# Loads of three stages issued one stage ahead, and the keys' bias rows written by ScalarE

## The reference, cut to what matters

```python
def even_mixer(h_lat, h_ctx, w_in, q_gain, k_gain, f_gain, w_fmix, w_out, cos, sin, need_ctx):
    q, ga, k, v, u, gb = jnp.split(h @ w_in, EVEN_SPLITS, axis=-1)   # for context and latents
    q, k = rms_norm(q, q_gain), rms_norm(k, k_gain)                   # 12 query heads, 4 key heads of 64
    ql, kl = apply_rope(ql, cos, sin), apply_rope(kl, cos, sin)
    attention: context on itself, latents on all 2304 keys
    fourier_mix: un = rms_norm(u, f_gain); fft2(un, axes=(1, 3)).real; per group @ w_fmix
    y = concat([a * silu(ga), f * silu(gb)]) @ w_out
x = layer_norm(ALPHA * x + g * y) * post_ln_gain + post_ln_bias
```

## Time and profile before

| | us |
|---|---|
| median of 3 runs | 3640.65 |
| lowest, highest | 3634.57, 3640.83 |
| the profiled execution, device time | 3631.57 |
| its span, first to last instruction | 3629.8 |
| heads stage in it | 574.4 to about 691 |
| Fourier stage in it | 1792.6 to about 1858.1 |
| mixer out, first instruction | 1858.34 |
| TensorE busy, share of the span | 93% |
| VectorE, GpSimd, ScalarE busy | 65%, 51%, 37% |

### The profile page before, as it was taken

How to read it: one execution, slowest core, us unless ns; L and a number is a source line. 1 busy time by engine, 2 the same in 40 slices (tenths; PEclk the granted TensorE clock), 3 DMA queues, 4 the chain that set the end, 5 groups by cost and what they waited for, 6 DMA issues and landing times. The chain is left out here.

```text
span 3629.8 us, 49706 instructions
## 1 busy us (share of the span) xinstructions
PE 3375.2 (93%) x16176; PEld 2487.3 (69%) x16176; DVE 2377.5 (65%) x3519; ACT 1348.9 (37%) x2266; POOL 1841.1 (51%) x1240
## 2 busy tenths in 40 slices
PE   7999997799999999999779899799999998999798
PEld 5788884555555555555368689687878786877587
DVE  4666533778777777777647654466575645777566
ACT  3423333444444444444320033334343423654200
POOL 1033305477777777777434334323586513444354
PEclk9999997899999999999889999999999999999899
DMA  5345437411111111111245455564545446677563
GB/s 211 110 117 141 132 92 222 149 33 35 35 35 35 36 39 38 35 35 35 80 151 176 158 179 175 197 199 147 171 132 171 146 148 213 210 225 241 195 221 137
DMA packets 358864, 475.35 MB, mean 131 GB/s; under 512 B 57964, under 2 KB 212476, under 8 KB 358544
## 3 DMA queue, kind: packets, MB, share of 16 engines
q1 hardware_dynamic: 299024, 357.32, 31.6%
q10 hardware_dynamic: 53200, 95.64, 8.7%
q0 software_dynamic: 6448, 19.94, 1.4%
HBM read 337.32 MB, written 135.36 MB: 130 GB/s over the span
## 5 line engine op out<-in xcount | busy, mean ns | idle before, releaser
L2371 DVE TENSOR_REDUCE al_mx<-al_sx 128x1 f32<-128x512 f32 (+1 forms) x960 | 559.7, 632 | 201.6 <-PE al_sx L2474 191.9
L2291 ACT ACTIVATE al_e<-al_st 128x1024 f32<-128x1024 f32 x432 | 443.3, 1027 | 535.3 <-PE al_st L2489 535.1
L2340 POOL TENSOR_TENSOR al_acc_p<-al_acc_p,al_e 128x1024 f32<-128x1024 f32 x188 | 455.5, 2423 | 19.5 <-POOL al_acc_p L2334 0.5
L274 PE MATMUL pb_acc<-p_whi,pb_r_hi 128*128 128x512 f32 x952 | 379.4, 398 | 39.7 <-DVE pb_r_lo L1708 28.8
L2498 PE MATMUL al_acc<-al_e,vres 128*64 128x512 f32 x1728 | 402.5, 601 | 0.0
L276 PE MATMUL pb_acc<-p_whi,pb_r_lo 128*128 128x512 f32 x952 | 376.7, 396 | 0.0
L275 PE MATMUL pb_acc<-p_wlo,pb_r_hi 128*128 128x512 f32 x952 | 376.0, 395 | 0.0
L1708 DVE TENSOR_TENSOR pb_r_lo<-pb_stg,pb_r_hi 128x512 fp32r<-128x512 f32 x238 | 249.8, 1053 | 166.9 <-ACT pb_r_hi L1606 162.6
L2488 PE MATMUL al_st<-al_qa,kres 128*128 128x512 f32 x864 | 346.8, 401 | 3.8 <-issue 3.2
L2489 PE MATMUL al_st<-al_qb,kres 128*128 128x512 f32 x864 | 341.0, 395 | 0.0
L2474 PE MATMUL al_sx<-kres,al_qx 128*128 128x512 f32 (+1 forms) x960 | 310.9, 397 | 8.8 <-DVE al_mx L2371 7.2
(11 more groups left out here) (345 smaller groups left out, 7384.8 us busy)
## 6 DMA issues: line engine op xcount, KB each, us to landing
pb_stg<-s_hsum ACTq DMA_DIRECT2D x238, 256.0 KB, 2.8
s_proj<-pb_out SPq DMA_DIRECT2D x72, 256.0 KB, 3.3
p_wst<-in_w1s ACTq DMA_DIRECT2D x18, 1024.0 KB, 5.8
ml_k<-s_proj SPq DMA_DIRECT2D x36, 512.0 KB, 4.4
ml_v<-s_proj SPq DMA_DIRECT2D x36, 512.0 KB, 8.8
hm_w<-in_ada_w SPq DMA_DIRECT2D x16, 1024.0 KB, 8.8
ml_qt<-s_qt SPq DMA_DIRECT2D x32, 512.0 KB, 6.4
s_h<-ml_h POOLq DMA_DIRECT2D x32, 512.0 KB, 8.2
```

The source lines that it names most:

```text
L274: nc.tensor.matmul(out, s_hi, m_hi, start=start, stop=False)
L2291: nc.scalar.activation(e[:, pair(p, j), :, :], st[(NP * p + j) % 2][:, :, 0:W], ACT.Exp).then_inc(e_done, 1)
L2340: nc.gpsimd.tensor_tensor(acc_p[:], acc_p[:], e[:, pair(p, j)], ALU.add).then_inc(add_p, 1)
L2371: V.tensor_reduce(mx[:, x:x + 1], slots[x % NSX][:, 0:spans[x % NS][1]], AX.X, ALU.max).then_inc(sx_max, 1)
```

## The change

Three objects now own inputs of a later stage, and their loads are issued in the stage before.

- `HeadInputs` lies at the right end of SBUF from the first stage on. Its weight ring `hm_w` takes the place of half 1 of the projections' `whi` and `wlo`, its raw rows that of the tile `x`, its gains and rope rows that of the query heads' `turn`. At k = 76 of the projections SP waits until the query heads are through with them (`tr_done`, `sq_done`, `px_done`, `ss_done`, `turn_done`) and for `mm_done` of chunk 3, and loads the gains; from k = 76 to 83 it loads, in turn, 4 tiles of raw and rope rows and 4 pieces of `ada_w`.
- In the heads stage SP starts with the modulation's constants and the first context queries. The gains are no longer loaded by ScalarE's queue.
- GpSimd's `bias_rows` is gone. ScalarE writes the 8 half rows as copies of one column of the identity, 2 in each of rounds 0, 1, 2 and 1 in each of rounds 3, 4, ahead of `high_part`.
- `FourierInputs`: SP loads `u` in one DMA and all tables before the last pair of stores of the attention.
- In the Fourier stage the scratch tiles `ep`, `em`, `op`, `om` lie in the mixer's input tile and `side` lies in `four`; the output weights get 3 slots instead of 2, and their high parts begin at y = 3. SP loads the mixer's first two tiles (`MixerInputs`) after `odd_done`, between output weights 2 and 3.
- Mixer out starts without the four loads of its first two tiles.

```diff
@@ class HeadInputs (new)
+        with ExitStack() as shared:
+            self.split = [shared.enter_context(nc.sbuf_tensor(n, [P, KD, CH], F32R, side="right"))[:] for n in ("pj0_whi1", "pj0_wlo1")]
+        self.w = right("hm_w", [P, self.ROWS, KD // 2, CH])
+        self.x = right("hd_x", [P, 3 * D])
+    def load_rows(self, eng, n):
+        i = n % self.ROWS
+        eng.dma_start(self.raw[:, i, :], self.s["proj0"][n * P:(n + 1) * P, QW:C_GATE]).then_inc(self.ld[i], 16)
+        eng.dma_start(self.rope[:, i], self.a["rope"][n * P:(n + 1) * P]).then_inc(self.ld[i], 16)
@@ projections, SP
+                n = k - (K - 14)
+                if n == 0:
+                    for done, count in ((hq.tr_done, NT), (hq.sq_done, NT), (hq.px_done, NT), (hq.ss_done, NT), (hq.turn_done, 2 * NT)):
+                        sp.wait_ge(done, count)
+                    sp.wait_ge(mm_done, last_of[NCH - 2] + 1)
+                    head.load_gains(sp)
+                if 0 <= n < 8 and n % 2 == 0:
+                    for i in (NT + n // 2, 2 * NT + n // 2):
+                        sp.wait_ge(stored[i % NST], 16 * (i // NST) + 16)
+                    head.load_rows(sp, n // 2)
+                elif 0 <= n < 8:
+                    l, c = HEAD_CHUNKS[n // 4]
+                    head.load_weights(sp, n // 2, (l, c, n // 2 % 2))
@@ heads, SP
-            load(0)
             sp.dma_start(mod.sel[:], a["mod_sel"]).then_inc(mod.const, 16)
             sp.dma_start(mod.sil[:], s["sil"]).then_inc(mod.const, 16)
+            ca.load(sp, 0)
             for n in range(NR_RAW):
-                if n:
-                    load(n)
                 mod.load(sp, n)
-            ca.load(sp, 0)
@@ heads, ScalarE
+            def bias_rows(i):
+                at = i % 2 * (T // 2)
+                nc.scalar.activation(kres[HD:P, NKV + i // 2, at:at + T // 2], keep["ident"][HD:P, HD:HD + 1].broadcast_to([P - HD, T // 2]), ACT.Copy).then_inc(rows_done, 1)
-            act.dma_start(gk[:], a["qk_gain"][:, QW:QW + HD].broadcast_to([P, HD])).then_inc(gain_ld, 16)
-            act.dma_start(gf[:], a["f_gain"].broadcast_to([P, FW])).then_inc(fgain_ld, 16)
             squares(0)
             for n in range(NT):
                 if n + 1 < NT:
                     squares(n + 1)
+                for i in ((0, 1), (2, 3), (4, 5), (6,), (7,))[n] if n < 5 else ():
+                    bias_rows(i)
                 if n:
                     high_part(n - 1)
@@ heads, GpSimd
-            def bias_rows(h, i):
-                x = kres[:, NKV + h, i * (T // 2):(i + 1) * (T // 2)].bitcast(F32)
-                nc.gpsimd.memset(x[HD:P], 0.0).then_inc(rows_zero, 1)
-                pool.wait_ge(rows_zero, 2 * h + i + 1)
-                nc.gpsimd.memset(x[HD:HD + 1], 1.0).then_inc(rows_done, 1)
@@ attention, SP
             over_blocks(sp, body)
+            following.load(sp)
             store(TOTAL - 2, TOTAL // 2 - 1)
@@ class FourierInputs (new)
+        sp.dma_start(self.u[:], self.s["un"].rearrange("(t p) n -> p t n", p=P)).then_inc(self.u_ld, 16)
+        sp.dma_start(self.small[:, 0:2, :], self.a["dft_head"].rearrange("c p n -> p c n")).then_inc(self.small_ld, 16)
+        sp.dma_start(self.small[:, 2:4, :], self.a["fmix"].rearrange("c p n -> p c n")).then_inc(self.small_ld, 16)
+        sp.dma_start(self.tabs[0][:], self.a["dft_ctx"]).then_inc(self.small_ld, 16)
+        sp.dma_start(self.tabs[1][:], self.a["dft_lat"]).then_inc(self.tab_ld, 16)
@@ fourier, SP
-            sp.wait_ge(u_ld, 48)
-            sp.dma_start(tabs[1][:], a["dft_lat"]).then_inc(tab_ld, 16)
-            for k in range(2):
+            for k in range(out_weights.depth):
                 out_weights.load(sp, k)
-            for k in range(2, KD):
+            sp.wait_ge(odd_done, 1)
+            for i in range(2):
+                mixer.load(sp, i, slice(i * P, (i + 1) * P))
+            for k in range(out_weights.depth, KD):
                 out_weights.load(sp, k)
@@ fourier, ScalarE
-                if y >= 4 and k < KD:
+                if y >= 3 and k < KD:
@@ mixer_out, SP
             def before():
-                inputs(0, 0, 0)
-                inputs(1, 1, 0)
+                if not L0:
+                    inputs(0, 0, 0)
+                    inputs(1, 1, 0)
                 constants()
@@ program
-    out_weights, four = OutWeights(nc, m, 0, a["w_out0"], 2), m.sb("four", [P, 2, T])
+    out_weights, four, mixer_in = OutWeights(nc, m, 0, a["w_out0"], 3), m.sb("four", [P, 2, T]), MixerInputs(m, s)
```

More of the change, by code:

```diff
@@ L197, with __init__ @@
+HEAD_CHUNKS = [(0, 4), (0, 5)] + [(1, c) for c in range(6)]
 class FirstInputs:
-    def __init__(self, m, a):
-        self.a = a
+    def __init__(self, m, a, head):
+        self.a, self.head = a, head
         self.hall = m.sb("pj0_hall", [P, KD, NT, P])
         self.wst = m.sb("pj0_wst", [P, KD // 2, CH])
-        self.x = m.sb("pj0_x", [P, 3, D])
+        self.x = head.rows
         self.w1_st = self.hall[:, 0:KD // 2, NT - 4:, :].rearrange("p k t n -> p k (t n)")
@@ L700, in _ @@
                 hq.load_gain(sp)
-            for k, (c, t) in enumerate(steps):
+            for k, (_, t) in enumerate(steps):
+                c = steps[k][0]
                 if c == 0 and t == 0:
@@ new lines, with __init__, load @@
+class MixerInputs:
+    def __init__(self, m, s):
+        self.s = s
+        self.ins = m.sb("mo0_in", [P, 2, 2, D])
+        self.in_ld = m.sem("mo0_in_ld", 2)
+        self.sems, m.sems = m.sems, []
+    def load(self, sp, p, rows):
+        sp.dma_start(self.ins[:, p, 0, 0:QW].rearrange("p (k n) -> p k n", n=P), self.s["attn"][:, rows].rearrange("(k p) n -> p k n", p=P)).then_inc(self.in_ld[p], 16)
+        sp.dma_start(self.ins[:, p, 1, :].rearrange("p (k n) -> p k n", n=P), self.s["gt"][:, rows].rearrange("(k p) n -> p k n", p=P)).then_inc(self.in_ld[p], 16)
@@ L2587, in fourier @@
+def fourier(nc, m, a, s, keep, out_weights, four, early, mixer):
     jobs = ((0, CT, "dft_ctx"), (CT, LT, "dft_lat"))
     H, Q = LT // 2, LT // 4
-    u = m.sb("fo_u", [P, NT, FW])
+    u, small, tabs = early.u, early.small, early.tabs
+    m.sems += early.sems
     ev, od = m.sb("fo_ev", [P, H - 1, FW]), m.sb("fo_od", [P, H - 1, FW])
-    ep, em, op, om = (m.sb("fo_" + x, [P, Q - 1, FW]) for x in ("ep", "em", "op", "om"))
-    side = m.sb("fo_side", [P, 14, FW])
+    ep, em, op, om = (mixer.ins[:, i // 2, i % 2, 0:(Q - 1) * FW].rearrange("p (t n) -> p t n", n=FW) for i in range(4))
+    sides = [four[:, i // 9, i % 9 * FW:(i % 9 + 1) * FW] for i in range(14)]
@@ L2782, in _, with mixer_out @@
                 mixed(n)
-def mixer_out(nc, m, a, s, keep, layer, out, out_weights, following=None, four=None):
+def mixer_out(nc, m, a, s, keep, layer, out, out_weights, following=None, four=None, early=None):
     L0 = layer == 0
@@ L2830, in inputs @@
                     sp.wait_ge(y_done[p], v)
-                elif not (isinstance(n, int) and n < 2):
+                else:
                     sp.wait_ge(lo_done, n - 1)
```

146 lines of the change are left out of this document (83 added, 63 removed).

## The result

The changed kernel takes 3605.7 us (median of 5 runs, 3598.7 to 3616.4), the kernel before 3640.8 in the same comparison: a ratio of 0.9914, 95% interval 0.990 to 0.9928. The forecast was 3602, and 3587 to 3616 its range. The profiled execution of after took 3605.7 with a span of 3604.0; that of before had a span of 3629.8, on a run (3631.6) 9 us under its kernel's median. So the two profiles differ by 25.8 us where the medians differ by 35, and the forecast's own sum, −38.2 between profiles, was 12 us too large.

A forecast was written before the change was run, and what follows sets the result against it. TensorE fills 93% of the span, so gains lie in late stage starts and heads' early rounds. Heads −18, attention +0.5, Fourier −15, mixer −5.7 give −38.2 us: 3593.4 profiled, 3602 as median, range 3587 to 3616.

The forecast's parts named there:

- What bounds the kernel: TensorE fills 93% of the span; late starts in heads, Fourier and mixer out lie on the path.
- Heads, start: −4.1: Start of heads: inputs are there at opening, so ScalarE's first copy comes 4.1 us earlier.
- Heads, rounds 0 to 5: 21.3 us: Heads: without GpSimd's memsets rounds follow ScalarE, scalings running from 580.1 to 601.4; round 5 comes 20.7 us earlier.
- Heads, rounds 5 to 17: 64 us: Heads: 58 us at VectorE's pace, plus 5 for TensorE's low clock (0 to 10) and 1 for DMA engines (0 to 5).
- rival B: Heads: low clock in rounds 2 to 8 and 2.1 us bias copies leave −8, 3612; chance 0.25 together with the DMA rival.
- my own sign for B: Heads: scalings in rounds 5 to 12 over 5.5 us apart, with TensorE back to back at 1.2 GHz.
- Projections: 0: Last 14 projection steps: 6 MB of added loads and the wait at k = 76 cost nothing.
- rival D: Last 14 projection steps: loads ahead of stores stall TensorE each step, making the kernel slower by over 0.2%; chance 0.02.
- End of attention: +0.5: End of attention: last store waits behind five loads of 4.98 MB, costing 0.5 us, bounds 0 and 3.
- Fourier −15.0 and mixer −5.7: Fourier: earlier start and output weights, −15.0 us; mixer out: first product 0.3 us after start instead of 6.0, −5.7.
- the tail −20.2: Terms after heads: end of attention +0.5, Fourier −15, mixer out −5.7.

The follow-up runs named there:

- heads_late: Changed kernel with gains, row tiles 0 to 3, their ropes and weight pieces 0 to 3 loaded when heads opens again: 3615.5 us, ratio 0.9949 to the kernel before.
- before_rows_act: Kernel before with only the bias rows moved from GpSimd's memsets to ScalarE copies, all loads left in place: 3632.2 us, ratio 0.9991 to the kernel before.
- aligned128: Changed kernel with 96 unused bytes at the right end of SBUF: 3597.9 us, ratio 0.9889 to the kernel before.
- before_shifted: Kernel before with 32 unused bytes ahead of whi and wlo of the first projection, no load moved: 3647.2 us, ratio 1.003 to the kernel before.

## Why the prediction was right, and where its steps were not

- **What bounds the kernel.** Right: all three places lay on the path, and what they gave arrived at the end. The end moved by 25.8 us where the first matmul of mixer out had moved by 25.1.
- **Heads, start: −4.1.** Right: −3.7 between profiles; 5.5 in `heads_late`.
- **Heads, rounds 0 to 5: 21.3 us.** Mis-sized: 26.5 to 26.8 in the six profiles of after's order. The price of a copy was right (1.1 us). I had counted ScalarE's load but not what stood behind the copies: a key copy that VectorE needs, and a modulation row that TensorE needs while it is at 1.2 GHz. These two sit in the intervals that were off: 5.9 us instead of 3.3 from round 1 to 2, and 8.4 instead of 5.4 from 3 to 4. With the copies behind these, and TensorE's idle time filled, the five rounds took 22.2.
- **Heads, rounds 5 to 17: 64 us.** Measured 63.5 in the profiled run, and 59.6 to 70.1 in others, so the match of this one profile is luck. The floor was right (59.1), TensorE's low clock goes with 0.5 to 11 us by the run against my bounds of 0 to 10, and no cost of the DMA engines showed. What failed is the idea that before's own profile had little of it by nature: its 10 us of low clock is at the lower end of what this stage shows. Of rival B the clock is real and sits in every run to a different degree: in after itself three rounds took 6.4 to 7.3 us with TensorE busy 84 to 94% of them at a clock of 0.73 to 0.77, which comes near my own sign for B. Its bias copies at 2.1 us did not come.
- **Projections: 0.** The step that failed. Loads, stores and the wait at k = 76 indeed cost nothing (TensorE has no gap there); rival D fell with them. But I costed only what the change moves in time and not what it moves in space: the matmuls of two chunks read tiles at new addresses. In numbers, 18 x 24 matmuls x 6.6 ns and 18 x 24 x 7.4 ns, 6.1 us; the steps' start times give 5.6. The other 3.0 us of the 8.6 are there at 80 us, and `before_rows_act`, with before's code up to there, is 2.3 us later than before at the same point: so most of them are spread between runs.
- **End of attention: +0.5.** Not seen. The last store is issued at 1785.9, 14.8 us after the first of the five loads, and lands within 2.4 us like the others. The last load, issued about 1776.5 and landed 10.6 us later, was all but through by then: from 1780 to 1785 the DMA engines moved 428 GB/s, where I had taken 317. So the case that I took from the Trainium skill ("DMA: Bandwidth & Descriptors", section "Queues, rings and completion order"), a store held back by the rest of a large load, did not arise, and no run here tests that rule. SyncE's lines in after:

```profile
1771.06 0.59 SPq L2639 DMA_DIRECT2D fo_u<-s_un  x1
...
1776.18 0.43 SPq L2643 DMA_DIRECT2D fo_dft_lat<-in_dft_lat  x1
1785.40 1.11 SPq L2288 DMA_DIRECT2D s_attn<-al_o  x2
```

- **Fourier −15.0 and mixer −5.7, with the tail −20.2.** Right: measured −21.1. The first sum came 10.7 us earlier against 10.8 in the forecast; the output weights, 4.2 in it (15.0 − 10.8), are worth 3.8.

Two errors of 5.5 us each and the 3 us of spread, less just under 2 us that the other terms gave beyond the forecast, made the sum between profiles 12 us too large. That the time still came within 4 us of the forecast is in part luck: the profiled run of before was 9 us under its median, and I had carried that distance over to after, whose profiled run lay at its median. The mechanism was right for the three places; the number came closer than the sum deserved.

## What to carry to other kernels

When an edit moves or splits a tile that TensorE reads, compare the matmuls' distance from start to start before and after, by the tile they read: 7 ns in 227 is invisible in any wait and still ate 5.6 of 35 us here, and 96 unused bytes bought it back (`aligned128`: 5.5 us less in the projection, and 3597.9 against 3608.3 for after on the same chip). When work is moved onto an engine with slack, look at which results stand behind it in that engine's order, not only at its busy time. And where TensorE's clock falls in a stage, read that stage from several executions before giving its microseconds to an edit.

## What the runs showed of the hardware

- Matmuls of 128x512 in fp32r follow each other at 226.8 ns with some start addresses of their two operands and at 229 to 234.2 with others; 32 bytes were enough to change it (`before_shifted`). The kernel before had this too: one product in seven of the second projection ran at 234. The Trainium skill, page "SBUF — State Buffer", section "Operand start alignment", says of its rule that an operand may start at any multiple of its element size: "This is about legality, not speed". These runs give the speed side: up to 3%.
- The same program had 10 and 31 us of TensorE at 1.2 GHz in the same twelve rounds of two executions, and took 63.5 and 70.0 us for them. In the second it was busy all of a 9.4 us round at the lower level.
- What one profile shows as gained can be given back by the clock: the bias rows alone took 7.5 us off rounds 0 to 5, rounds 5 to 17 came out 10.7 us longer with 29 us at 1.2 GHz, and over the timed runs the kernel was 0.1% faster.
